# Norm and gate rows as TensorE products of one small tile instead of broadcast loads

## The reference, cut to what matters

```python
for l in range(2):                              # first block
    mod = silu(c) @ ada_w[l] + ada_b[l]         # sh1, sc1, g1, sh2, sc2, g2
    h = modulate(x, sh1, sc1)                   # layer norm without gain
    mix = hybrid_mixer(h)                       # attention, convolution, stick-breaking
    x = layer_norm(ALPHA * x + (1 + g1) * mix, ln1_g[l], ln1_b[l])
    ffn = peer(modulate(x, sh2, sc2))           # 128 of 16384 experts for each token
    x = layer_norm(ALPHA * x + (1 + g2) * ffn, ln2_g[l], ln2_b[l])
for i in range(2):                              # second block: latent and context tokens
    x_mid = x + g1 * rmsnorm(mix, norm_post_mix[i])
    x = x_mid + g2 * rmsnorm(swiglu(...), norm_post_ffn[i])
    # in layer 0 the 256 context tokens take the same path, with gates of their own
```

## Time and profile before

| | us |
|---|---|
| runs | 2892.09, 2902.78, 2904.34 |
| median | 2902.78 |
| profiled execution | 2893.22 |
| its span | 2891.4 |
| TensorE products busy | 1891.9 |
| VectorE busy | 1803.3 |
| POOL busy | 1071.4 |
| ScalarE busy | 374.6 |

### The profile page before, as it was taken

The page is one execution under the profiler, slowest core; times in us unless marked ns, Lnnn a source line. Parts: engine busy times, 40 slices in busy tenths (PEclk is TensorE's granted clock), DMA queues, the critical chain, the costliest instruction groups (busy, mean ns, idle before and its releaser), DMA issues.

```text
span 2891.4 us, 23615 instructions
## 1 busy us (share of the span) xinstructions
PE 1891.9 (65%) x8197; PEld 1332.9 (46%) x8197; DVE 1803.3 (62%) x3281; ACT 374.6 (13%) x830; POOL 1071.4 (37%) x1047
## 2 busy tenths in 40 slices
PE   7889444185644363454364467767188999988998
PEld 4668111064342151142251156643157786477873
DVE  1436999889678889979889986676944200142001
ACT  1311001022102010002011000000014100131000
POOL 1002444577355555755556765465600000000000
PEclk8989556586776685776678788889579999999999
DMA  8366999999999999999999999999860544512443
GB/s 288 111 217 226 399 399 401 369 376 374 371 402 404 400 401 391 336 368 399 399 403 374 339 348 392 368 405 405 323 237 30 189 150 156 189 61 90 157 146 116
DMA packets 359975, 860.86 MB, mean 298 GB/s; under 512 B 23721, under 2 KB 146865, under 8 KB 359729
## 3 DMA queue, kind: packets, MB, share of 16 engines
q0 software_dynamic: 148288, 538.12, 48.4%
q1 hardware_dynamic: 211568, 321.24, 31.9%
HBM read 858.23 MB, written 1.05 MB: 297 GB/s over the span
## 4 chain that ended last, share of the span: by engine, by line
PE 36%; DMA 33%; DVE 14%; issue 11%; POOL 3%; ACT 2%; SPq 0%; DVEq 0%; ACTq 0%
PE bank L927 13%; DMA RING<-in_peer_v,EX 10%; PE bank L415 8%; DMA W<-in_w_ada 6%; PE bank L941 5%; DMA W<-in_ada_w 4%; DMA RING<-in_peer_u,EX 3%; PE bank L424 3%; DMA WORK<-in_peer_u,EX 3%; DMA W<-in_w_up 2%; DVE ACC L1680 2%; POOL RING L1041 2%; PE bank L447 2%; DMA W<-in_w_gate 2%; DMA WORK<-in_peer_v,EX 2%
## 5 line engine op out<-in xcount | busy, mean ns | idle before, releaser
L927 PE MATMUL bank<-HT,W 128*128 128x256 f32 x2112 | 482.0, 392 | 61.6 <-DMA W<-in_w_up 30.3
L927 PEld LDWEIGHTS bank<-HT,W 128*128 128x128 f32 x2112 | 414.8, 197 | 128.6 <-DMA W<-in_w_up 33.9
L1041 POOL DMA_INDIRECT RING<-in_peer_u,EX x343 | 326.4, 952 | 378.8 <-DVE ACC L1662 244.7
L1662 DVE SCALAR_TENSOR_TENSOR ACC<-RING,hrows 128x1024 bf16<-128x1024 f32 x343 | 406.2, 1217 | 79.9 <-DMA RING<-in_peer_u,EX 77.6
L1041 POOL DMA_INDIRECT RING<-in_peer_v,EX x341 | 379.2, 1112 | 206.6 <-DVE hrows L1680 91.5
L447 PE MATMUL bank<-W,CACT 128*32 128x512 f32 x704 | 149.9, 955 | 237.5 <-DMA W<-in_w_ada 135.3
L403 PE MATMUL bank<-consts,XN 128*128 128x128 f32 x208 | 44.6, 397 | 312.4 <-DVE XN L1505 144.6
L415 PE MATMUL bank<-W,HT 128*128 128x256 f32 x992 | 228.7, 394 | 18.6 <-ACT HT L1101 7.4
L941 PE MATMUL bank<-W,WORK 128*128 128x512 f32 x528 | 229.3, 597 | 14.4 <-DVE WORK L2279 14.4
L1041 POOL DMA_INDIRECT WORK<-in_peer_v,EX x171 | 193.7, 1133 | 100.1 <-DVE hrows L1680 39.2
L2279 DVE TENSOR_TENSOR WORK<-WORK,bank 128x256 f32<-128x256 f32 x66 | 27.2, 420 | 321.3 <-ACT WORK L1401 321.3
(11 more groups left out here) (356 smaller groups left out, 2332.1 us busy)
## 6 DMA issues: line engine op xcount, KB each, us to landing
W<-in_w_ada SPq DMA_DIRECT2D x48, 1024.0 KB, 16.4
W<-in_ada_w SPq DMA_DIRECT2D x40, 1024.0 KB, 12.9
W<-in_w_gate SPq DMA_DIRECT2D x33, 1024.0 KB, 5.5
W<-in_w_up SPq DMA_DIRECT2D x33, 1024.0 KB, 5.6
W<-in_w_down SPq DMA_DIRECT2D x33, 1024.0 KB, 5.0
W<-in_w_in SPq DMA_DIRECT2D x32, 1024.0 KB, 13.6
W<-in_peer_wq SPq DMA_DIRECT2D x22, 1024.0 KB, 17.4
W<-in_w_out SPq DMA_DIRECT2D x12, 1024.0 KB, 5.3
```

The source lines that it names most:

```text
L927: mm = pe.matmul(bs[j][:, g * S:(g + 1) * S], w[:, k, j * P:(j + 1) * P], HT[:, k, :], start=(k == 0 and g == 0), stop=(k == DC - 1 and g ...
L1041: gp.indirect_dma_start(SLOT[g % NS], None, rows, bass.IndirectOffsetOnAxis(EX[:, t, k:k + 1], 0))\
L1662: ve.scalar_tensor_tensor(out=JUNK[:, g % 2, :], in0=SLOT[g % NS], scalar=1.0, in1=HB[:, :], op0=ALU.mult, op1=ALU.mult, accum_out=ACTS[:, ...
```

## The change

Twenty rows are read once, 4 KB each, into partitions 0 to 19 of a tile `ROWM`, by ten loads on POOL's queue behind the first projection product of block 0. `spread_into` multiplies `ROWM` by a broadcast column of the identity, so that a bank holds one half row in all 128 partitions. `spread` makes the four half rows of a pair for VectorE. For gate biases the product is added to the gate product in its own bank. Two full broadcasts for `ln1` of block 0 also go through POOL's queue, into `HN` and `ACC`, and one pair for the last `ln2` still goes through SyncE's, into `HN` and `GA[:, 3]`.

```diff
@@ tensor
+            def spread_into(b, kind, l, hf, start):
+                r = ROW_AT[kind] + l
+                return pe.matmul(b[:, :], ident[0:NROWS, r:r + 1].to_broadcast([NROWS, P]), ROWM[0:NROWS, hf * 512:(hf + 1) * 512],
+                                 start=start, stop=True)
+
+            def spread(name, kind, l):
+                for hf in range(2):
+                    b = open_bank((*name, hf), "V")
+                    spread_into(b, kind, l, hf, True).then_inc(filled, 1)
@@ ada
+                    if kind not in kinds:
+                        continue
                         pe.matmul(b[:, :], const("who")[:, who:who + 1].to_broadcast([P, P]), ROWT[:, half, :],
-                                  start=True, stop=True).then_inc(filled, 1)
+                                  start=True, stop=False)
+                        spread_into(b, ("ada_" if p[0] == "b" else "ada2_") + "12"[(q - 8) // 2], int(p[1]), q % 2, False)\
+                            .then_inc(filled, 1)
@@ block1, tensor
-                load_rows(d["ada_b"][l][2 * D:3 * D], d["ada_b"][l][5 * D:6 * D])
...
-                ada(p, aw, [0], GATE1)
+                pe.wait_ge(row_vectors, 16 * 10)
+                ada(p, aw, [0], GATE1, kinds=("mr",))
...
                 wo = d["w_o"][l].rearrange("(k p) n -> p k n", p=P)
+                ada(p, aw, [0], GATE1, kinds=("mc",))
                 pe.wait_ge(mark("co", p), 1)
...
-                load_rows(d["ln1_g"][l], d["ln1_b"][l])
...
-                for c in range(DC):
-                    mm = pe.transpose(HB[:, c * P:(c + 1) * P], HT[:, c, 0:P], ident)
-                mm.then_inc(mark("first", p), 1)
-                for hf in range(2):
-                    transposes(("hn", p, hf), "A", [HT[:, 4 * hf + j, P:2 * P] for j in range(4)])
...
+                    if (what, n) == score_order[2]:
...
@@ tile1, tensor
-                load_rows(d["ada_b"][l][2 * D:3 * D], d["ada_b"][l][5 * D:6 * D])
...
-                load_rows(d["ln1_g"][l], d["ln1_b"][l])
+                spread(("ln1", p, t, 0), "ln1_g", l)
+                spread(("ln1", p, t, 1), "ln1_b", l)
@@ block2, tensor
-                    load_rows(d["b_ada_2"][1][5 * D:6 * D], d["norm_post_ffn_2"][1])
...
-                    load_rows(d["b_ada_2"][1][2 * D:3 * D], d["norm_post_mix_2"][1])
                 yield
                 modulated(p, 2, 2, VA)
+                if who == "l":
+                    spread(("post", "l1", l), ("post_mix", "post_ffn")[l], 1)
@@ the order of the work, tensor
-            load_rows(d["b_ada_2"][0][2 * D:3 * D], d["b_ada_2"][0][5 * D:6 * D])
             ada("b1", d["ada_w"][1], [0], FIRST, beside=lambda i: gather(0, 0, 0, 10 * i + 64))
-            load_rows(d["norm_post_mix_2"][0], d["norm_post_ffn_2"][0])
+            spread(("post", "c0", 0), "post_mix", 0)
+            spread(("post", "c0", 1), "post_ffn", 0)
...
             ada("b1", d["ada_w"][1], [0], SECOND)
-            load_rows(d["ln2_g"][0], d["ln2_b"][0])
+            spread(("ln2", "b0", 0, 0), "ln2_g", 0)
+            spread(("ln2", "b0", 0, 1), "ln2_b", 0)
             tile1(1, 0)
-            load_rows(d["ln2_g"][0], d["ln2_b"][0])
...
             tile1(1, 1)
-            load_rows(d["ln2_g"][1], d["ln2_b"][1])
...
...
-            load_rows(d["ln2_g"][1], d["ln2_b"][1])
+            load([(HN[:, :], d["ln2_g"][1].partition_broadcast(P)), (GA[:, 3, :], d["ln2_b"][1].partition_broadcast(P))],
+                 rows_landed, (mark("dots", "b1"), 2))
@@ gpsimd
+            gp.wait_ge(filled, banks["ql", "b0"][0] + 1)
+            for name, (src, c0) in {...}.items():
+                gp.dma_start(ROWM[ROW_AT[name]:ROW_AT[name] + 2, :], d[src][:, c0:c0 + D]).then_inc(row_vectors, 16)
+            gp.dma_start(HN[:, :], d["ln1_g"][0].partition_broadcast(P)).then_inc(wide_rows, 16)
+            gp.dma_start(ACC[:, :], d["ln1_b"][0].partition_broadcast(P)).then_inc(wide_rows, 16)
@@ scalar
+                            if p[0] == "b":
+                                b = wait_full(act, name)
+                                free(name, A(dst, b[:, :], ACT.Identity, bias=const("one")))
...
+                gate1 = ada(p, [0], GATE1)
+                next(gate1)
                 for t in range(NT):
                     act.wait_ge(mark("smax", p), t + 1)
...
-                all_of(ada(p, [0], GATE1))
+                next(gate1)
...
+                all_of(gate1)
...
-            for _ in range(22):
-                next(early)
-            act.wait_ge(mark("gated", "b0"), 1)
             all_of(early)
...
-            all_of(ada("b1", [0], SECOND))
+            second = ada("b1", [0], SECOND)
+            for _ in range(3):
+                next(second)
+            root1("b0", 0, 5)
+            all_of(second)
@@ vector
-            def scaled_rows(p, t):
+            def scaled_rows(kind, p, t):
                 inverse(p, t)
+                for i, scalar in enumerate((MV, RSD)):
+                    for hf in range(2):
+                        c = slice(hf * 512, (hf + 1) * 512)
+                        b = wait_full(ve, (kind, p, t, i, hf))
+                        free((kind, p, t, i, hf), ve.scalar_tensor_tensor(
+                            out=X[:, t, c], in0=X[:, t, c], scalar=scalar[:, t, 0:1], in1=b[:, :],
+                            op0=(ALU.subtract, ALU.mult)[i], op1=(ALU.mult, ALU.add)[i]))
+                    settle()
...
-                do(ve.scalar_tensor_tensor(out=g, in0=g, scalar=1.0, in1=ROWS[:, t, :], op0=ALU.add, op1=ALU.add), rows_read)
...
-                rows_here()
-                do(ve.tensor_copy(GA[:, 4, :], ROWS[:, 1, :]))
@@ gate_rows (c0) and gate_row (l0, l1)
+                            ins = ve.tensor_tensor(GA[:, gs[half], c], GA[:, gs[half], c], b[:, :], ALU.mult)
...
-            stage(0, 0, 1, {k: [c0] for k in (0, 3, 5, 10, 16, 20, 22, 26, 30)})
+            stage(0, 0, 1, {k: [c0] for k in (0, 3, 8, 14, 18, 20, 24, 29)})
...
-                stage(t, 1 - t, 0, {k: [a] for k in (0, 1, 4, 11, 12, 14, 16, 17, 19, 23, 28)})
+                stage(t, 1 - t, 0, {k: [a] for k in ((0, 1, 4, 12, 13, 15, 17, 18, 20, 24, 29),
+                                                     (0, 1, 4, 11, 12, 14, 16, 17, 19, 23, 28))[t]})
...
-            stage(1, 1, 0, {0: [a], 1: [c0], **{8 + (13 * i) // 5: [c0] for i in range(9)}})
+            stage(1, 1, 0, {0: [a], 1: [c0], **{9 + (14 * i) // 5: [c0] for i in range(9)}})
```

More of the change, by code:

```diff
@@ L619, in block1 @@
                         scores(*n)
+                    if (what, n) == score_order[2]:
+                        for c in range(DC):
+                            mm = pe.transpose(HB[:, c * P:(c + 1) * P], HT[:, c, 0:P], ident)
+                        mm.then_inc(mark("first", p), 1)
+                        for hf in range(2):
+                            transposes(("hn", p, hf), "A", [HT[:, 4 * hf + j, P:2 * P] for j in range(4)])
                 ada(p, aw, [0], GATE2)
@@ L1117, in ada @@
                             at = GATES[p, who][(q - 8) // 2]
-                            copy(("ga", p, who, (q - 8) // 2, q % 2), GA[:, at, (q % 2) * 512:(q % 2 + 1) * 512])
+                            name, dst = ("ga", p, who, (q - 8) // 2, q % 2), GA[:, at, (q % 2) * 512:(q % 2 + 1) * 512]
+                            if p[0] == "b":
+                                b = wait_full(act, name)
+                                free(name, A(dst, b[:, :], ACT.Identity, bias=const("one")))
+                            else:
+                                copy(name, dst)
                     yield
@@ L1186, in block1 @@
                     copy(("kk", p, i), SKT[:, 4 * i:4 * i + 4, :], lambda b: b[:, :].rearrange("p (u n) -> p u n", u=4))
-                for hf in range(2):
-                    copy(("hn", p, hf), HN[:, hf * 512:(hf + 1) * 512])
                 for what, n_ in score_order:
@@ L1196, in block1 @@
                     copy(("ps", p, t, i), SS[l, t][:, 4 * i:4 * i + 4, :], lambda b: b[:, :].rearrange("p (u n) -> p u n", u=4))
+                    if n_ == (0, 0):
+                        for hf in range(2):
+                            copy(("hn", p, hf), HN[:, hf * 512:(hf + 1) * 512])
                 all_of(ada(p, [0], GATE2))
@@ L1758, in tile1 @@
                 w, n = (t + 1) * 512, (t + 1) * P
-                scaled_rows(f"b{l - 1}", t)
+                scaled_rows("ln2", f"b{l - 1}", t)
                 moments(p, t)
@@ L1870, in tile1 @@
                 yield
-                scaled_rows(p, t)
+                scaled_rows("ln1", p, t)
                 moments(p, t)
@@ L1889, in block1 @@
                 finish_mod(p, p, l, 0, False, 0)
-                def finish_gate(half, bias, s):
-                    wait_empty(ve, *[("ga", p, 0, half, hf) for hf in range(2)])
-                    g = GA[:, gs[half], :]
-                    do(ve.scalar_tensor_tensor(out=g, in0=g, scalar=1.0, in1=bias, op0=ALU.add, op1=ALU.add), s)
```

(14 more changed lines are left out.)

74 lines of the change are left out of this document (38 added, 36 removed).

## The result

In sixteen executions of each kernel the median went from 2896.39 to 2909.59 us, a ratio of 1.0042 (95% interval 1.0029 to 1.0056). Weighted by runs the two are 1.0036: about **10.3 us slower**, within half a per cent, where the prediction's sum had 20.5 us faster. A ratio's interval is 0.0009 to 0.0017 to either side, 3 to 5 us, so a difference of two is known to some 4 to 6 us.

What follows compares the result with a forecast made beforehand. Transfers and VectorE were taken to bound the middle part by turns, TensorE the latent passes. Terms -21.0 - 5 - 3.5 + 1 - 1.7 + 9.7 = -20.5 us from 2893.22 gave 2872.7; with run scatter 2878, range 2856 to 2902.

Steps and rivals of the forecast that it cites:

- Bytes: Middle part: nine broadcast pairs fewer at 400 GB/s, 2.6 us each for seven and half for two, -21.0 us.
- Block 0's attention: Block 0: gate products moved behind the values, later exponentials, four products ahead of the transposes, +1 us (-1 to +6).
- The context pass and the first row scaling: Context pass: new plan and root moved ahead cut both waits from 20.2 to 14 to 15 us, -5 us.
- The latent passes: Both latent passes: spread products ahead of the feed-forward and in the gates lengthen TensorE's path, +9.7 us (7.5 to 12.6).
- VectorE: Context pass gate rows as half rows from a bank -4.3 us, five row scalings in halves +0.8, sum -3.5 us.
- Routing: HB and HN transposes moved behind the first scores, so the first gather starts earlier, -1.7 us.
- The ten small and two wide loads on POOL's queue: Block 0: all twelve loads out by 85 us, under 55 us of cover, cost nothing.
- Rival 3: Spread products come late behind weight passes, VectorE waits at five row scalings, +34 us in all: +21.4, 2915 us; chance 0.08.
- rival 1: VectorE sets the pace and saved bytes only leave transfers idle: +0.5, 2894 us; chance 0.30.
- rival 2: A broadcast pair costs 4.7 us, so the bytes save 42 us instead of 21: 2852 us; chance 0.12.

Runs made afterwards that it cites:

- e4: The kernel before the change, with its nine row pairs of the middle part loaded over 8 columns of 1024: 0.9950 of the kernel before, 2877.38 us.
- e2: The changed kernel with ScalarE's copy of the first product row of block 0's first gate behind its exponentials again: 0.9995 of the kernel before, 2891.65 us.
- the first execution: The first profiled execution of the unaltered changed kernel: span 2912.5 us.
- e1: The changed kernel with the first row scaling's four spread products moved inside block 1's modulation product: 0.9993 of the kernel before, 2890.04 us.
- e8: The changed kernel with the context pass's steps in the rounds of the plan before the change: 1.0020 of the kernel before, 2899.54 us.
- e3: The changed kernel with the latent passes' gate rows loaded as broadcast pairs as before, without spread products there: 0.9991 of the kernel before, 2891.2 us.
- e11: The changed kernel with its three losses undone and block 1's second root ahead, but the HB and HN transposes ahead of the query products: 0.9909, 2863.47 us.
- e6: The changed kernel with first-scaling spreads inside the modulation product, block 0's copy behind the exponentials, its products between output products, latent gate rows loaded: 0.9908, 2868.75 us.
- the second profiled execution: The unaltered changed kernel profiled again in a second set of runs: span 2902.3 us, ratio of that set 1.0027.

## Why the prediction was wrong

The sum was -20.5 us, the measured change +10.3. Term by term:

- **Bytes, -21.0: right in kind, too large.** e4 measures -14.5. The step that failed is "in a full stretch VectorE waits for gathers, so all of it counts": in e4's profile VectorE's waits for gathers did fall by 20 us, but the time only by 14.5. The share of 9 holds in slices of both sorts, those bound by transfers and those bound by VectorE, so it doesn't tell which pair lies where the transfers end the wait. That only a part of the nine did is the reading that fits; no run tried the pairs one by one.
- **Block 0's attention, +1 (bounds -1 and +6): wrong by 11 us.** e2 measures 11.9 us for the copy alone. The exponentials' end was worked out rightly (9.6 us behind the start of TensorE's modulation product, and 9.5 us in the profile). So was what they leave, 4.5 us later less the 3.4 of the gate products: counted from that product, the values begin 1.1 us later (14.0 us behind it for 12.9). The step that failed is the clock of what follows: "3.4 us at full clock against a gap of 0.9, thus +2.5", and the values taken as they were. TensorE waited twice for the late exponentials, with the gate products that had stood there moved away, and then the values took 2.7 us more and the four products 8.0 us against the gap of 1.0, so +7.0. 1.1 + 2.7 + 7.0 are the 10.8 us of the profile.
- **The context pass and the first row scaling, -5: the sign is wrong.** The step "the row scaling now waits for four spread products ... at half clock 1.71 us each, 6.8 us" prices the products and not what stands ahead of them. Before, the 5.8 us were a wait for the root behind the modulation product. The change took the root from behind it, and put the rows there. The wait kept its cause, the late weights, and got 7.2 us of products on top. Residual and row scaling together waited 25.9 us (28.1 in the first execution), where 20.2 were read before and 14 to 15 forecast. e1 measures 12.4 us for the place of the products. The residual's wait did fall (14.4 to 9.5, and 4.1 in the first execution), but by e8 this alone was worth nothing.
- **The latent passes, +9.7 (bounds 7.5 to 12.6): too small, and by luck not smaller.** e3 measures 13.0. Two steps were off, in opposite directions: there are two spread products ahead of each feed-forward part, not four; and a product costs 1.05 us at full clock (in e2 four products of 512 columns take the 4.16 us from 156.91 to 161.07) and 1.8 to 2.0 at half, for the 0.86 and 1.71 taken from long runs of products. What else stands beside them at half clock, such as the transposes (3.32 us for 1.91), was no term of the sum.
- **VectorE, -3.5.** Not tried by itself. The context pass's gate rows took 0.68 us each as forecast, but a row scaling's half took 0.75 and not 0.68: +2.1 for +0.8.
- **Routing, -1.7.** The first gather moved by 1.3 to 1.6 us (e11); in the time e11 can't tell it from nothing.
- The ten small and two wide loads on POOL's queue were issued by 62.2 us, and the profile shows no wait for them, as forecast.

The four measured terms come to -14.5 + 11.9 + 12.4 + 13.0 = +22.8 us, 12.5 more than the change cost. e6 says the same: with the three losses undone the kernel is 26.6 us below the one before, 12.1 more than the bytes of e4. The other terms of the prediction (-5 - 3.5 - 1.7 = -10.2) would nearly fill this, but none of them was measured by itself in the changed kernel, and e8 found nothing in the plan. Where these 12 us come from stays open.

**The rivals.** Rival 3 had one of the three mechanisms, spread products behind whole weight passes. Its time (2915 us) is the nearest to the median of 2909.59, but by the change (+10.3) its +21.4 is no nearer than rival 1's +0.5. It reckoned with 34 us at five places; it was 16 to 24 us at one. The reason held against it, that at four of five VectorE comes late anyway, was right; for the fifth the prediction reads no row for when TensorE would be free, though the trace of before has it (the row of 772.28 us above). No case held the front's loss in full (the term's bound was +6). Rival 1 fell with e4, rival 2 as well. The sum starts from the fast end of three runs, 2893; this was no error, since the median of before stood at 2896 in the comparison and at 2890 to 2894 in the sets after it.

The Trainium skill's VectorE: DVE Perf Modes, in its section on the TRN2 errata, gives a matmul 6 cycles and its columns, from which the prediction estimated 0.43 us for such a product. The rows show 1.05 us, still further from it than the prediction's 0.86, and they decide.

## What to carry to other kernels

When a wait is taken away, ask which late thing it waited for, and whether what replaces it stands behind the same thing in another engine's queue; price the place in the queue and not the instructions. A copy moved ahead makes everything behind it in its engine wait for what the copy waits for; where TensorE idles because of that, the lower clock of what follows can cost more than the wait. Products that replace idle transfers, as in the latent passes here, only add time: cut bytes only where transfers end the waits, and there expect a part of what the rate would give.

## What the runs showed of the hardware that was not expected

- Two short waits went with a long stretch at the lower clock. In the front TensorE idled for 2.07 and 2.14 us ahead of the stretches at 0.62 and 0.50; in e2, which has one wait of 0.56 us in their place, the clock was 1.00 in all stretches from 138 to 180 us. Before, one wait of 2.06 us stood there; the clock was 0.50 at 148 to 150 us and mostly full again in the next stretch:

```profile
150.00:158.00 8.00, 7.12 (x56) 6.29 (x54) 2.77 (x4) 2.39 (x4) 0.00 (x0) 0.91 0.06 18
```

- A product of 20 partitions by 512 columns takes 1.05 us at full clock and 1.8 to 2.0 at half, as long as one of 128 partitions beside it (1.12 and 1.08 in e2's rows).
- In one execution TensorE got its instructions one or two at a time, 0.7 to 2.8 us from start to start, for 42 us, while gathers had 95% of the transfers' time and the weights' queue 8%:

```profile
q0 software_dynamic: 4679, 17.03, 95.0%
q1 hardware_dynamic: 677, 1.33, 7.8%
```

These are the queues from 825 to 870 us there (packets, MB, share); in the second profiled execution it was 70% and 33% in the same stretch. None of the twelve executions profiled after it shows such a stretch. What starved it stays open.
